# V products alternating between column groups, attention with the probabilities as stationary operand, and two smaller moves on VectorE

## What is computed

```python
def attend(q, k, v):                       # 8 query heads, 2 key/value heads, head size 64, 1280 keys
    s = einsum('bqkgd,bskd->bkgqs', q, k) * HEAD_DIM ** -0.5
    p = softmax(s, axis=-1)
    return einsum('bkgqs,bskd->bqkgd', p, v)

def one(xc):                               # one chunk of 128 tokens, 8 chunks
    q = (xc @ wq).reshape(128, 8, 2, 128)
    s = einsum('nhpd,hpkd->nhpk', q, subkeys)
    s1, i1 = top_k(s[:, :, 0], 16);  s2, i2 = top_k(s[:, :, 1], 16)
    cand_s = s1[..., :, None] + s2[..., None, :]
    cand_i = i1[..., :, None] * 128 + i2[..., None, :]
    top_s, pos = top_k(cand_s, 16);  idx = take_along_axis(cand_i, pos)
    g = softmax(top_s)
    act = gelu(einsum('nhkd,nd->nhk', u[idx], xc))
    return einsum('nhk,nhkd->nd', g * act, v[idx])
```

## Time and profile before

| | |
|---|---|
| median of 3 runs | 3096.01 us (3094.7 to 3098.4) |
| the profiled execution | 3099.57 us, of which the span of the core's instructions is 3097.7 us |
| PE busy | 2520.1 us, 81% |
| DVE busy | 2142.4 us, 69% |
| POOL busy | 2102.9 us, 68% (without the 0.30 us between two gathers) |
| ACT busy | 819.6 us, 26% |
| granted TensorE clock | 0.901 of full speed over the span |
| DMA | 1163.76 MB, 376 GB/s over the span |

### The profile page before, as it was taken

One profiled execution on the slowest core, in us unless ns is written; L12 is line 12 of the kernel. 1 busy time (PEld: TensorE's weight loads), 2 busy tenths in 40 slices (PEclk: granted clock), 3 DMA queues, 4 the chain that ended last, 5 costly groups with the idle time before them and its releaser, 6 DMA issues.

```text
span 3097.7 us, 29161 instructions
## 1 busy us (share of the span) xinstructions
PE 2520.1 (81%) x9190; PEld 1107.2 (36%) x9190; DVE 2142.4 (69%) x4677; ACT 819.6 (26%) x1848; POOL 2102.9 (68%) x2167
## 2 busy tenths in 40 slices
PE   6978998697788878897789878988888788733598
PEld 4844466333333333323232433233333333211122
DVE  4787587977777776778767877867777777566400
ACT  2358222123212321232223321322123212100122
POOL 5930044667777777777777777777777777777775
PEclk9988999798989998999899888989898989876799
DMA  9532278999999999999999999999999999999998
GB/s 343 177 149 83 92 282 297 407 372 407 415 419 419 419 419 416 419 409 415 418 420 400 419 419 419 416 414 418 411 419 408 419 407 418 419 420 420 411 419 353
DMA packets 335937, 1163.76 MB, mean 376 GB/s; under 512 B 40485, under 2 KB 51365, under 8 KB 333608
## 3 DMA queue, kind: packets, MB, share of 16 engines
q0 software_dynamic: 297792, 1084.36, 86.6%
q1 hardware_dynamic: 37994, 77.54, 7.1%
HBM read 1148.13 MB, written 13.63 MB: 375 GB/s over the span
## 4 chain that ended last, share of the span: by engine, by line
PE 31%; DMA 26%; POOL 18%; DVE 13%; issue 7%; ACT 3%; SPq 1%; DVEq 0%; POOLq 0%; ACTq 0%
POOL arena L608 18%; PE psum L2041 15%; DMA arena<-in_u,idx_u 15%; DMA arena<-in_v,arena 11%; DVE arena L1536 7%; PE psum L1974 3%; PE psum L1752 2%; PE psum L1930 2%; PE psum L1908 1%; PE psum L1903 1%; PE psum L1862 1%; PE psum L1689 1%; PE psum L1915 1%; PE psum L1890 1%; PE psum L1849 1%
## 5 line engine op out<-in xcount | busy, mean ns | idle before, releaser
L2041 PE MATMUL psum<-arena 128*32 128x512 f32 x4096 | 1312.2, 668 | 303.1 <-DMA arena<-in_v,arena 291.9
L1536 DVE CUSTOM_DVE_ANT_0 arena<-arena,psum 128x1024 f32<-128x1024 f32 x1024 | 1230.4, 1219 | 441.7 <-DMA arena<-in_u,idx_u 427.9
L608 POOL DMA_INDIRECT arena<-in_u,idx_u x1024 | 973.5, 951 | 460.5 <-issue 224.6
L608 POOL DMA_INDIRECT arena<-in_v,arena x1024 | 980.3, 957 | 338.8 <-issue 258.5
L2041 PEld LDWEIGHTS psum<-arena 128*32 128x32 f32 x4096 | 378.2, 118 | 1173.5 <-issue 1033.6
L937 ACT ACTIVATE arena<-arena 128x32 f32<-128x32 f32 x1024 | 308.3, 318 | 1234.1 <-PE psum L2041 1232.7
L1974 PE MATMUL psum<-wbig,arena 128*128 128x512 f32 x512 | 230.7, 605 | 1.1 <-ACT arena L899 1.1
L1862 PE MATMUL psum<-kT,arena 64*128 64x512 f32 (+1 forms) x384 | 171.5, 584 | 32.2 <-ACT arena L814 24.6
L1890 PE MATMUL psum<-arena,v 128*64 128x128 f32 x1120 | 147.3, 291 | 26.5 <-ACT arena L861 26.5
L1881 PE MATMUL psum<-ident,arena 128*128 128x128 f32 x560 | 102.9, 300 | 59.3 <-ACT arena L861 44.0
L1890 PEld LDWEIGHTS psum<-arena,v 128*64 128x64 f32 x1120 | 133.8, 147 | 40.2 <-ACT arena L861 40.2
(11 more groups left out here) (265 smaller groups left out, 2180.9 us busy)
## 6 DMA issues: line engine op xcount, KB each, us to landing
arena<-in_u,idx_u POOLq DMA_INDIRECT x1024, 8.6
arena<-in_v,arena POOLq DMA_INDIRECT x1024, 8.8
arena<-in_w_mod POOLq DMA_DIRECT2D x20, 512.0 KB, 5.2
wbig<-in_wq SPq DMA_DIRECT2D x1, 7168.0 KB, 19.8
arena<-in_w_mod SPq DMA_DIRECT2D x12, 512.0 KB, 5.0
arena<-in_xin SPq DMA_DIRECT2D x5, 1024.0 KB, 9.1
arena<-in_w_mod SPq DMA_DIRECT2D x2, 2048.0 KB, 10.6
wbig<-in_w_mod SPq DMA_DIRECT2D x2, 2048.0 KB, 20.5
```

Of the source, the lines that this page charges most:

```text
L608: pool.indirect_dma_start(ring[:, r, :], None, t[table], bass.IndirectOffsetOnAxis(idx[:, j:j + 1], 0)).then_inc(got[r], 16)
L1536: V.tensor_tensor_reduce(ring[:, r, :], ring[:, r, :], hx_cur, 1.0, 0.0, ALU.mult, ALU.add, act_[:, j:j + 1]).then_inc(S["u_used"], 1)
L2041: ins = M(bank(4 + b)[QP * q:QP * q + QP, :], lhsT=sel[:, j % SELS, :], rhs=ring[:, r, 512 * b:512 * b + 512], start=(i == 0), stop=(i == ...
```

## The change

It has five parts.

1. `v_slots`: the two products of a slot go to two column groups, bank 4 to group q and bank 5 to group (q + 2) % 4. The sum in bank 5 then stands shifted by 64 rows, and `move_sum` copies it in three pieces in place of one.
2. `attention`: `pr` isn't divided any more. DVE only inverts the sum (`invert_sum`). The product with the values has the block of `pT` (128x128) as stationary operand and the values (128x64) as the moving one. The result stands with the tokens across the partitions, so that ACT can scale it by the inverse sum as it moves it to `tok` (`move_tok`). Two heads fill `tok`; PE turns it once for each pair (`turn_pair`) and ACT moves it to `att` (`move_pair`). For pairs 0 to 2 both steps stand in the third group of the turning of heads 2, 4 and 6; pair 3 is turned at the start of `post`, and its product is put last in the output projection.
3. `retrieve`: the two number lists of the sub-keys are first combined with their places (`near` = 256 x place + number, two passes over 128x64), and two passes over 128x1024 are left for each sub-key (subtract, and the minimum of the absolute value) in place of three.
4. `MIX_FIRST`, `XM_FIRST`: 88 and 92 in place of 96 and 102.
5. PE's turning of a head waits for the exponentials (`probs_ready`) in place of `probs_normed`.

The core of the diff:

```diff
-MIX_FIRST, XM_FIRST = 96, 102
+MIX_FIRST, XM_FIRST = 88, 92
...
+            def move_tok(n, h, pv):
+
+                o, b = HD * (h % 2), 46 + h % 2
+                act.wait_ge(S["sum_inverted"], n * NQ + h + 1)
+                A(tok[:, o:o + HD], pv, ACT.Copy, scale=small[:, b:b + 1]).then_inc(S["tok_ready"], 1)
+
+            def move_pair(n, i):
+
+                if i == 3:
+                    act.wait_ge(S["pair_turned"], n + 1)
+                A(att[:, i, :], pair_at(n, i), ACT.Copy).then_inc(S["att_ready"], 1)
...
+                        if g == 2 and h % 2 == 0 and h:
+                            move_pair(n, h // 2 - 1)
                         A(pT[:, 4 * g:4 * g + k, :], bank(3)[:, 0:k * P], ACT.Copy).then_inc(S["pt_out"], 1)
...
-                    A(att[o:o + 64, h // 2, :], bank(3)[0:64, 0:P], ACT.Copy).then_inc(S["att_ready"], 1)
+                    move_tok(n, h, bank(3)[:, 0:HD])
...
-                A(ff, ffn, ACT.Copy).then_inc(S["ffn_out"], 1)
+                A(ff[:, 0:512], bank(4), ACT.Copy)
+                A(ff[0:64, 512:D], bank(5)[64:P, :], ACT.Copy)
+                A(ff[64:P, 512:D], bank(5)[0:64, :], ACT.Copy).then_inc(S["ffn_out"], 1)
...
-            def normalise(n, h):
+            def invert_sum(n, h):
 
                 b = 46 + h % 2
                 dve.wait_ge(S["probs_ready"], n * NQ + h + 1)
-                ch.link(V.reciprocal(small[:, b:b + 1], small[:, b:b + 1]))
-                V.tensor_scalar(pr, pr, small[:, b:b + 1], None, ALU.mult).then_inc(S["probs_normed"], 1)
+                V.reciprocal(small[:, b:b + 1], small[:, b:b + 1]).then_inc(S["sum_inverted"], 1)
...
+                for p_ in range(2):
+                    ch.step(V.scalar_tensor_tensor(near[:, p_], iota16[:, :].unsqueeze(1).broadcast_to([P, 4, TOPK]),
+                                                   float(LABEL), ixu[:, hs, p_, :], ALU.mult, ALU.add))
...
                 for p_ in range(2):
-                    ch.link(V.tensor_tensor(
-                        oneh.rearrange("p h k a -> p (h k) a"),
-                        pab[:, p_].rearrange("p h k -> p (h k)").unsqueeze(2).broadcast_to([P, 4 * TOPK, TOPK]),
-                        iota16[:, :].unsqueeze(1).broadcast_to([P, 4 * TOPK, TOPK]), ALU.is_equal))
-                    ch.link(V.tensor_tensor(oneh, oneh, ixu[:, hs, p_, :].unsqueeze(2)
-                                            .broadcast_to([P, 4, TOPK, TOPK]), ALU.mult))
-                    ch.link(V.tensor_reduce(selv[:, p_], oneh, AX, ALU.add))
+                    ch.link(V.tensor_tensor(oneh, near[:, p_].unsqueeze(2).broadcast_to([P, 4, TOPK, TOPK]),
+                                            pab[:, p_].unsqueeze(3).broadcast_to([P, 4, TOPK, TOPK]), ALU.subtract))
+                    ch.link(V.tensor_reduce(selv[:, p_], oneh, AX, ALU.min, apply_absolute_value=True))
...
-                    pe.wait_ge(S["probs_normed"], n * NQ + h + 1)
-                    pe.wait_ge(S["att_ready"], n * NQ + h)
+                    pe.wait_ge(S["probs_ready"], n * NQ + h + 1)
+                    pe.wait_ge(S["tok_ready"], n * NQ + h)
+                    if h:
+                        wait(pe, "att_ready", 4 * n + (h - 1) // 2)
...
+                        if g == 2 and h % 2 == 0 and h:
+                            ins = turn_pair(n, h // 2 - 1)
                         ins.then_inc(S["pt_ready"], 1)
...
-                        ins = M(pv, lhsT=v[:, kt, 64 * (h % 2):64 * (h % 2) + 64], rhs=pT[:, kt, :],
+                        ins = M(pv, lhsT=pT[:, kt, :], rhs=v[:, kt, 64 * (h % 2):64 * (h % 2) + 64],
                                 start=(kt == 0), stop=(kt == NTOK - 1))
...
+                    turn_pair(n, 3).then_inc(S["pair_turned"], 1)
+                    pe.wait_ge(S["att_ready"], 4 * n + 3)
...
                     for b in range(2):
-                        ins = M(bank(4 + b)[QP * q:QP * q + QP, :], lhsT=sel[:, j % SELS, :],
+                        g = (q + 2 * b) % QUADS
+                        ins = M(bank(4 + b)[QP * g:QP * g + QP, :], lhsT=sel[:, j % SELS, :],
                                 rhs=ring[:, r, 512 * b:512 * b + 512], start=(i == 0), stop=(i == QP - 1))
```

More of the change, by code:

```diff
@@ L59 @@
 SELS = 8
+LABEL = 2 * NK
 EPS = 1e-6
@@ L285, in first_pv, with pair_at @@
         def first_pv(h):
-            return bank(6 + h % 2)[0:64, 2 * P:3 * P]
+            return bank(6 + h % 2)[:, 2 * P:2 * P + HD]
+        def pair_at(n, i):
+            if n == 0:
+                return bank(7 if i == 3 else 6)[:, 3 * P:4 * P]
+            return bank(3)[:, 2 * P:3 * P]
         def similar(u, i):
@@ L1387, in attention @@
                     fill(first_norm + every * h)
-                    normalise(n, h)
+                    invert_sum(n, h)
                     if h + 1 < NQ:
@@ L1593, in _ @@
                 a = 2 * f
-                normalise(0, a)
+                invert_sum(0, a)
                 if f + 2 < LF:
@@ L1601, in _ @@
                     lru_in(a + 2)
-                    normalise(0, a + 1)
+                    invert_sum(0, a + 1)
                 else:
@@ L1826, in turn_probs, with turn_pair @@
                     ins = T(bank(6 + l % 2)[:, j * P:(j + 1) * P], pr[:, kt * P:(kt + 1) * P], ident[:, :])
+                if g == 2 and h % 2 == 0 and h:
+                    ins = turn_pair(0, h // 2 - 1)
                 ins.then_inc(S["pt_ready"], 1)
+            def turn_pair(n, i):
+                pe.wait_ge(S["tok_ready"], n * NQ + 2 * i + 2)
+                return T(pair_at(n, i), tok, ident[:, :])
             def values(h):
@@ L1930, in out @@
                     return M(bank(i), lhsT=att[:, kt, :] if kt < 4 else lc[:, kt - 4, :],
-                             rhs=wo[:, kt, 512 * i:512 * i + 512], start=(kt == 0), stop=(kt == KT - 1))
+                             rhs=wo[:, kt, 512 * i:512 * i + 512], start=(kt == 0), stop=(kt == 3))
                 if n == 0:
-                    for kt in (2, 7, 3):
-                        out_first(kt)
+                    out_first(2)
+                    turn_pair(0, 3).then_inc(S["pair_turned"], 1)
+                    out_first(7)
+                    out_first(3)
                 else:
```

45 lines of the change are left out of this document (26 added, 19 removed).

## The result

The changed kernel takes 3110.28 us (3109.59 to 3111.66, 6 runs) against 3096.02 us of the kernel before (6 runs): ratio 1.0041, 95% interval 1.0031 to 1.0052, 10 to 16 us slower. The forecast was 25 us faster. The profiled execution has a span of 3109.7 us, 12.0 more than before.

What follows compares the result with a forecast made beforehand. From 650 us DMA engines were taken as nearly full (416 of 420 GB/s), with PE's V slots holding up POOL. Chunk 1 -10, steady part -15, end -0.5 gave -25.5 us: 3071 from 3096.0, range 3058 to 3089.

Steps and rivals of the forecast that it cites:

- So the cost stays: Products with the values: 0.12 us an instruction before, about 0.114 after; bounds 0.06 to 0.25.
- the term for chunk 1, -10: Chunk 1's attention and norms, head included: PE's chain and POOL's 12th V gather meet near 634 us instead of 644.30.
- The clock rival: In the loop, PE's granted clock falls as it has less to do, giving 3186 us; chance 0.06.
- The steady part, -15 us: After 644 us, V slots in alternating column groups take about 0.85 us instead of 1.241, cutting POOL's waits for PE.
- PE, once behind, cannot catch up: Last chunk, only V slots left: PE busy throughout at 1.241 us a slot, the same as POOL's pitch.
- the DMA rival: Steady stalls lie under a full DMA queue, so only chunk 1 and the end gain: 3085.5 us; chance 0.22.
- Norms, -7.5 us: Chunk 1's norms: PE's two waits fall from 15.9 to 8.4 us; DVE waits about 4 us at slot 88.
- The rest of chunk 1, -1.8 us: Chunk 1's attention: head 7's wait for normalise gone, -2.7, half clock after it -0.6, turned pairs +1.3 and +0.2.
- Two passes, 0: Sub-key numbers in retrieve: 2.2 us less DVE work each, 4.5 a chunk, but 0 on the path.
- head, -1.1: Head of the program: normalise out of the wait chain twice, -1.6 us, pair turning and copy added, +0.4 and +0.1.
- tail, -0.5: End of the last chunk: PE falls only one slot behind the last landing, -0.4 to -1.6; move_sum gives 0.6 back.
- pT's load, +20 us: Rival: loading pT does not hide, +2.5 us a head, +20 in chunk 1's 8 heads, 3090.5 us; chance 0.05.

Runs made afterwards that it cites:

- e5: Changed kernel with each product with the values taking all 128 columns of v, ACT copying the head's 64: 3089.51 us, ratio 0.9970.
- e9: Changed kernel with the 128-column product with the values in chunk 1 alone, 64 columns in the other chunks: 3088.16 us, ratio 0.9974.
- e3: Kernel before with only the V slots in alternating column groups and move_sum in three pieces: 3096.78 us, ratio 0.9996.
- e13: Changed kernel with 128-column values, V slots in one column group per slot again and move_sum in one piece: 3089.26 us, ratio 0.9972.
- e4: Kernel before with only chunk 1's norms moved to slots 88 and 92 from 96 and 102: 3093.15 us, ratio 0.9985.
- e14: Kernel before with only the new attention, its values 128 columns wide: 3097.82 us, ratio 1.0000.
- e2: Changed kernel with the attention of before put back, all other parts kept: 3091.26 us, ratio 0.9987.

## Why the prediction was wrong, step by step

Two terms of the sum failed. Gather 139 was forecast for 634 us, and came at 656.86, 23 us late; e5, with nothing changed but the width of the values, has it at 635.14, so nearly all of that is what the values cost. The part after it was to be 15 us shorter and was 0.2 longer: 15 us, from the value of V slots in alternating groups. The first alone turned a gain into a loss.

**The values.** "So the cost stays", 0.12 us an instruction, was the step that failed, and with it the term for chunk 1, -10, that held nothing for it. It was read in the head of the program, at the full clock, where it holds: 2.34 to 2.44 us for the 20 of the last heads of chunk 0 in the changed kernel. In chunk 1 the kernel before took 3.98 to 4.15 us for them (one head 3.83), so the trace of before showed a clock that falls inside the values of each head and comes back just in time for the scores. The change lets it come back later. The term was worth 18.5 us on PE (142.0 against 123.5) in the one stretch where PE's list sets the time.

**The clock rival.** I had one, with a chance of 0.06, but placed in the loop, and decided by how little PE has to do there. The loop's clock did fall (0.92 to 0.84) and cost nothing (e9). The fall that cost time was in chunk 1's attention, where PE's list has few pauses, and for which the text had no clock rival.

**The steady part, -15 us.** It was 0 (e3, e13 and the last column of the table). Two readings failed. "PE, once behind, cannot catch up" took the 1.241 us of the earlier trace rows for PE's own cost of a slot. But the last line of the earlier trace rows has 44 instructions, 11 slots that had all landed, in 5.76 us: 0.52 a slot. The busy time of the earlier trace rows is that of slots that come one in 1.243 us, and overlap was there already. And POOL's excess waits for PE did not hang on PE's work, as they stayed when PE waited 164 us longer for landings (e3). In its outcome that is the DMA rival, which had 0.22; whether the DMA engines or POOL's own pace of 1.243 us is the bound stays open. V slots paced by landings keep PE 75 of 90 us busy instead of 90, 84% where the forecast had 69%.

**Norms, -7.5 us.** Right: -7.6 on PE in e4, and the waits of 4.54 and 3.76 in the changed kernel. DVE's wait, 4 us in the forecast, was 11.1 as the projection ended 17.8 us later; the text had named "over 8 us at slot 88" as a sign that it was wrong. To the time the norms alone gave 4.6 us.

**The rest of chunk 1, -1.8 us.** Right in kind: -3.3 on PE (e5, e14). Two heads take 34.3 us in e5 and 34.1 before (POOL's long stalls end at 505.85 and 540.12, and at 506.08 and 540.14), so turned pairs and the wider product cost about what the terms said, and the gain is at head 7, whose wait is gone.

**Chunk 1 as a whole, -10.** e5, which is the change with its clock held, gets 6.0 to gather 139 and a ratio of 0.9970, 9.3 us. The wait for V slots is gone there, but POOL now stands 3.11 and 2.88 us for DVE at the two norms, where before it stood once, 3.13. So with its clock held the change comes to 3087, near the DMA rival's 3085.5 and not to 3071.

**Two passes, 0; head, -1.1; tail, -0.5.** The first is consistent with e2 against e4. The first gather lay between 379.3 and 386.8 us in the profiled executions without an order that follows the edits, so the head's term can't be told. The tail was 0.7 shorter.

**pT's load, +20 us.** It hides at the full clock, as forecast. The time, 14 us above before, is not near that rival's 3090.5; that the 18.5 us on PE are near its 20 is chance, as the cause is another.

## What to carry to other kernels

Before exchanging the operands of a product, compare the columns that are multiplied with the columns that are loaded. Here products of 64 columns behind loads of 128 looked as busy in the profile as products of 128 and lost the clock. In a list that nothing hides it can pay to multiply columns that are thrown away. Read an instruction's cost in the stretch where it will stand, at the clock granted there, and take an engine's own pace from a place where its inputs wait for it, not from where it keeps step with a queue. Where variants with much less work on an engine show the same time between two landmarks, that engine is not the bound there, even if waits are put down to it.

## What the hardware showed that was not expected

- The granted clock from 460 to 560 us, by columns loaded and multiplied in the values: 128 and 64, 0.77 (PE busy 90%); 128 and 96, 0.83 (87%); 128 and 128, 0.90 (86%); 64 and 64, 0.90 (79%).
- Filling waits of 0.5 to 0.7 us with products of 512 and 256 columns held the clock through values of 128 columns (2.50 us instead of 4.13 for six heads), through values of 64 columns only for three (2.44 us, the other five 4.53).
- A gather into 112 of 128 partitions, one in two of all gathers, brought the mean from 416 to 272 GB/s from 650 us on, at a DMA share of 0.97; one into 64 partitions 258 GB/s from 700 to 3500 us, at 0.96. The cause stays open.
